# A decoder trunk in fp32: the down projection's pairs in seven products take one weight row per slot, and late loads go in pieces

## What is computed

```python
D_MODEL, SEQ, D_FF = 2048, 256, 8192

h = rms_norm(x, norm_mix_pre)
...
x = x + rms_norm(mixed @ w_out, norm_mix_post)
h = rms_norm(x, norm_mlp_pre)
u = jnp.square(jax.nn.relu(h @ w_up))
x = x + rms_norm(u @ w_down, norm_mlp_post)
```

## Time and profile before

| | |
|---|---|
| median of 3 runs | 1708.07 us (1706.89 to 1712.73) |
| profiled execution | 1709.83 us, span 1708.5 us |
| granted TensorE clock, mean | 0.998 |
| TensorE busy | 1686.1 us (99%), 8444 matmuls |
| weight loads of TensorE | 1397.4 us (82%) |
| VectorE busy | 1094.4 us (64%) |
| ScalarE busy | 879.3 us (51%) |
| GpSimd busy | 55.6 us (3%) |
| DMA | 341.12 MB, mean 200 GB/s; `w_down` loads: 128 of 512 KB, 4.6 us to landing |

### The profile page before, as it was taken

How to read it: one execution, slowest core, us unless ns; L and a number is a source line. 1 busy time by engine, 2 the same in 40 slices (tenths; PEclk the granted TensorE clock), 3 DMA queues, 4 the chain that set the end, 5 groups by cost and what they waited for, 6 DMA issues and landing times.

```text
span 1708.5 us, 23779 instructions
## 1 busy us (share of the span) xinstructions
PE 1686.1 (99%) x8444; PEld 1397.4 (82%) x8444; DVE 1094.4 (64%) x1508; ACT 879.3 (51%) x1318; POOL 55.6 (3%) x104
## 2 busy tenths in 40 slices
PE   9999999999999999999999999999999999999997
PEld 7888888888888888788888888887778888887886
DVE  6444456766655555565665667657878567568888
ACT  6444455766655655544344565445545444445553
POOL 1000011111100102000000000000000000000000
PEclk9999999999999999999999999999999999999999
DMA  8666665766666769668767656665556666666564
GB/s 267 197 188 185 193 189 146 197 174 169 173 176 186 207 207 299 189 184 291 272 202 237 216 184 185 189 183 184 194 187 210 198 186 186 187 231 199 187 204 146
DMA packets 169010, 341.12 MB, mean 200 GB/s; under 512 B 11488, under 2 KB 14512, under 8 KB 168144
## 3 DMA queue, kind: packets, MB, share of 16 engines
q1 hardware_dynamic: 163088, 319.27, 59.8%
q0 software_dynamic: 5696, 20.54, 5.1%
q10 hardware_dynamic: 128, 0.03, 0.0%
HBM read 329.21 MB, written 10.58 MB: 199 GB/s over the span
## 4 chain that ended last, share of the span: by engine, by line
PE 90%; DVE 5%; DMA 3%; issue 1%; ACT 0%; DVEq 0%; ACTq 0%
PE ps L1145 13%; PE ps L857 11%; PE ps L859 10%; PE ps L858 10%; PE ps L1147 6%; PE ps L672 6%; PE ps L674 6%; PE ps L673 6%; DMA raw<-in_w_down_dram 3%; PE ps L1181 3%; PE ps L1183 3%; PE ps L1182 3%; PE ps L1196 1%; PE ps L1197 1%; PE ps L1198 1%
## 5 line engine op out<-in xcount | busy, mean ns | idle before, releaser
L1758 DVE TENSOR_TENSOR w_lo<-raw,w_hi 128x1024 fp32r<-128x1024 f32 x524 | 635.8, 1224 | 476.6 <-ACT w_hi L1267 466.8
L1267 ACT ACTIVATE w_hi<-raw 128x1024 fp32r<-128x1024 f32 x547 | 575.7, 1057 | 574.7 <-PE ps L674 147.6
L1145 PE MATMUL ps<-h_all,w_hi 128*128 128x512 f32 x960 | 339.4, 399 | 0.0
L857 PE MATMUL ps<-w_hi,h_all 128*128 128x512 f32 (+1 forms) x800 | 314.6, 393 | 0.0
L859 PE MATMUL ps<-w_hi,h_all 128*128 128x512 f32 (+1 forms) x800 | 309.0, 386 | 0.0
L858 PE MATMUL ps<-w_lo,h_all 128*128 128x512 f32 (+1 forms) x800 | 308.7, 386 | 0.0
L1147 PE MATMUL ps<-h_all,w_lo 128*128 128x256 f32 x960 | 269.6, 281 | 0.0
L1145 PEld LDWEIGHTS ps<-h_all,w_hi 128*128 128x128 f32 x960 | 180.4, 188 | 45.0
L1147 PEld LDWEIGHTS ps<-h_all,w_lo 128*128 128x128 f32 x960 | 181.3, 189 | 0.1
L857 PEld LDWEIGHTS ps<-w_hi,h_all 128*128 128x128 f32 x800 | 150.2, 188 | 36.2 <-issue 7.5
L859 PEld LDWEIGHTS ps<-w_hi,h_all 128*128 128x128 f32 x800 | 150.1, 188 | 30.5
(11 more groups left out here) (357 smaller groups left out, 1941.4 us busy)
## 6 DMA issues: line engine op xcount, KB each, us to landing
raw<-in_w_in_dram SPq DMA_DIRECT2D x239, 512.0 KB, 3.9
raw<-in_w_down_dram SPq DMA_DIRECT2D x128, 512.0 KB, 4.6
raw<-in_w_up_dram SPq DMA_DIRECT2D x124, 512.0 KB, 4.2
raw<-in_w_out_dram SPq DMA_DIRECT2D x32, 512.0 KB, 4.1
bias<-bias_table POOLq DMA_DIRECT2D x72, 128.0 KB, 4.2
raw<-in_w_branch_b_dram SPq DMA_DIRECT2D x16, 512.0 KB, 5.7
raw<-in_w_branch_c_dram SPq DMA_DIRECT2D x16, 512.0 KB, 5.5
gate_dram<-stage SPq DMA_DIRECT2D x12, 512.0 KB, 6.3
```

The lines of the kernel that those rows point to most:

```text
L857: pe.matmul(acc, h_hi[:, kc, tok], w_hi[:, slot, k, 0:cols], start=kc == 0, stop=False)
L1145: pe.matmul(ps[:, bank + b, :], w_hi[:, j % RING, k, cols], h_all[:, kc, :, :].rearrange("p a n -> p (a n)"), start=kc == 0, stop=False)
L1267: act.activation(w_hi[:, slot, :, :], raw[:, slot, :, :], ACT.Copy).then_inc(sem("hi_ready"), 1)
L1758: dve.tensor_tensor(w_lo[:, slot, :, :], raw[:, slot, :, :], w_hi[:, slot, :, :].bitcast(F32), ALU.subtract).then_inc(sem("lo_ready"), 1)
```

## The change

The two units of a pair no longer hold a half of the columns each with both hidden rows, but one hidden row each with all 1024 columns (slot 2 the odd row, slot 3 the even one). The first sum needs slot 2 alone. Sums and plain rests are cut into smaller steps; the odd row's rest, in slot 2, counts `lo_ready` for the first unit of the pair, the rest of slot 3 for the second, and both `t_lo` count `t_lo_ready`. TensorE waits four times within a pair and does the three products with plain blocks first. For the first pair behind `up` both `t_lo` are made before `up_sum`. `mid_again` is loaded in eight pieces of 256 KB, one for each four units of `down(1, 0)`, and `gain_again` in four of 256 KB beside the first four. The first two gain products move from the slots of units 24 and 25 to those of 29 and 30. Blank lines are left out.

```diff
--- before.py
+++ after.py
@@ -563,10 +563,19 @@
             for c in range(2):
                 chunk(Pos(U0[f"up{h}"] + CH * c, 2 * CH, i), w_up_v, 0, CH, i * (2 * W) + (h * DFF // 2 + W * c))
+        def load_row(u, slot, view, kc, col):
+
+            sp.wait_ge(sem("lo_ready"), u.count(1 - RING))
+            sp.dma_start(raw[:, slot, :, :].rearrange("p k n -> p (k n)"), view[:, kc, col:col + 2 * W]).then_inc(
+                sem(f"raw_loaded{slot}"), 16)
+
         def down(h, part):
-            for j, (_, p, half) in enumerate(DOWN):
-                load(Pos(U0[f"down{h}"] + DOWN_UNITS * part + j), j % RING, w_down_v, 32 * h + 2 * p,
-                     2 * W * part + W * half)
+            for j, (seven_products, p, half) in enumerate(DOWN):
+                u = Pos(U0[f"down{h}"] + DOWN_UNITS * part + j)
+                if seven_products:
+                    load_row(u, j % RING, w_down_v, 32 * h + 2 * p + 1 - half, 2 * W * part)
+                else:
+                    load(u, j % RING, w_down_v, 32 * h + 2 * p, 2 * W * part + W * half)
         sp.wait_ge(sem("unit_used"), U0["out"])
         for j in range(RING):
@@ -650,9 +659,14 @@
             pool.dma_start(mid[:, t, :], x[0, t * P:(t + 1) * P, :]).then_inc(sem("x_again"), 16)
         pool.wait_ge(sem("mid_stored"), 16)
-        pool.wait_ge(sem("unit_used"), U0["down1"])
-        pool.dma_start(mid_again[:, :, :].rearrange("p t n -> p (t n)"), mid_dram).then_inc(sem("mid_back"), 16)
-        pool.dma_start(gain_again[:, :], bass.AP(norm_mlp_post.tensor, 0, [[0, P], [1, D]])).then_inc(sem("gain_loaded"), 16)
+        for t in range(2):
+            for b in range(4):
+                pool.wait_ge(sem("unit_used"), U0["down1"] + 4 * (4 * t + b))
+                cols = slice(W * b, W * b + W)
+                pool.dma_start(mid_again[:, t, cols], mid_dram[:, D * t + W * b:D * t + W * b + W]).then_inc(sem("mid_back"), 16)
+                if t == 0:
+                    gain = bass.AP(norm_mlp_post.tensor, W * b, [[0, P], [1, W]])
+                    pool.dma_start(gain_again[:, cols], gain).then_inc(sem("gain_loaded"), 16)
     @block.tensor
@@ -1201,18 +1215,21 @@
                 return product(seven_bank(h, number), a_hi, a_lo, b_hi, b_lo, n == 0, n == SEVEN - 1)
             low, high, odd = slice(0, P), slice(P, SEQ), 2 * p + 1
-            pe.wait_ge(sem("lo_ready"), U0[f"down{h}"] + DOWN_UNITS * part + 4 * n + 4)
-            own(1, u_hi[:, odd, low], u_lo[:, odd, low], w4_hi[:, 1, :], w4_lo[:, 1, :])
+            unit = U0[f"down{h}"] + DOWN_UNITS * part + 4 * n + 2
+            pe.wait_ge(sem("lo_ready"), unit + 1)
+            own(1, u_hi[:, odd, low], u_lo[:, odd, low], w4_hi[:, 0, :], w4_lo[:, 0, :]).then_inc(sem("unit_used"), 1)
+            pe.wait_ge(sem("lo_ready"), unit + 2)
+            product(sum_bank(h, 0, 0), u_hi[:, 2 * p, low], u_lo[:, 2 * p, low], w4_hi[:, 2, :], w4_lo[:, 2, :],
+                    False, False)
+            product(sum_bank(h, 1, 0), s_hi[:, n, 2, :], s_lo[:, n, 2, :], w4_hi[:, 3, :], w4_lo[:, 3, :],
+                    False, False).then_inc(sem("unit_used"), 1)
+            pe.wait_ge(sem("t_lo_ready"), 2 * number + 1)
             own(5, u_hi[:, odd, high], u_lo[:, odd, high], t_hi[:, 1, :], t_lo[:, 1, :])
             own(7, s_hi[:, n, 0, :], s_lo[:, n, 0, :], t_hi[:, 0, :], t_lo[:, 0, :]).then_inc(sem("t_used"), 1)
-            pe.wait_ge(sem("t_lo_ready"), number + 1)
+            pe.wait_ge(sem("t_lo_ready"), 2 * number + 2)
             own(6, s_hi[:, n, 1, :], s_lo[:, n, 1, :], t_hi[:, 2, :], t_lo[:, 2, :])
             product(sum_bank(h, 0, 1), u_hi[:, 2 * p, high], u_lo[:, 2 * p, high], t_hi[:, 3, :], t_lo[:, 3, :],
                     False, False).then_inc(sem("t_used"), 1)
-            product(sum_bank(h, 0, 0), u_hi[:, 2 * p, low], u_lo[:, 2 * p, low], w4_hi[:, 0, :], w4_lo[:, 0, :],
-                    False, False).then_inc(sem("unit_used"), 1)
-            product(sum_bank(h, 1, 0), s_hi[:, n, 2, :], s_lo[:, n, 2, :], w4_hi[:, 2, :], w4_lo[:, 2, :],
-                    False, False).then_inc(sem("unit_used"), 1)
         def down(h, part):
@@ -1656,16 +1673,16 @@
         def t_round(number, pair):
-            act.wait_ge(sem("t_sums"), 3 * number + 1 + 2 * pair)
+            act.wait_ge(sem("t_sums"), 4 * number + 2 + 2 * pair)
             act.activation(t_hi[:, 2 * pair:2 * pair + 2, :], t_sum[:, 2 * pair:2 * pair + 2, :], ACT.Copy).then_inc(
                 sem("t_hi_ready"), 1)
         def prepare(n):
-            if n - 1 in SEVEN_OF:
-                act.wait_ge(sem("raw_loaded3"), Pos(n).loads())
+            if n in SEVEN_OF:
+                act.wait_ge(sem("raw_loaded2"), Pos(n).loads())
                 act.wait_ge(sem("unit_used"), n + 1 - RING)
-                act.activation(w_hi[:, 3, 0, :], raw[:, 3, 0, :], ACT.Copy).then_inc(sem("hi_ready"), 1)
+                act.activation(w_hi[:, 2, 0, :], raw[:, 2, 0, :], ACT.Copy).then_inc(sem("hi_ready"), 1)
             else:
                 split(Pos(n), n % RING)
@@ -1693,7 +1710,7 @@
         def mix_first(h, part):
-            act.wait_ge(sem("unit_used"), U0[f"down{h}"] + DOWN_UNITS * part + SEVENS_END)
+            act.wait_ge(sem("t_used"), 2 * (12 * h + SEVEN * (part + 1)))
             act.wait_ge(sem("up_lo"), 8 * h + 8)
             act.wait_ge(sem("mix_v"), MIX_V[h][part])
             one = ps[:, seven_bank(h, 1), :]
@@ -2390,36 +2407,45 @@
                 dve.tensor_tensor(s_lo[:, part, :, :], s_sum[:, part, :, :], s_hi[:, part, :, :].bitcast(F32),
                                   ALU.subtract).then_inc(sem("s_lo_ready"), 1)
-        def weight_sums(n):
+        def first_sum(n):
             number = SEVEN_OF[n]
-            for b in range(2):
-                dve.wait_ge(sem(f"raw_loaded{2 + b}"), Pos(n + b).loads())
+            dve.wait_ge(sem("raw_loaded2"), Pos(n).loads())
             if number == 0:
                 dve.wait_ge(sem("mid_stored"), 16)
             wait(dve, sem("t_used"), 2 * number - 1)
             rows = plain_rows(raw)
-            dve.tensor_tensor(t_sum[:, 0:2, :], rows[:, 2:4, :], rows[:, 3:0:-2, :], ALU.subtract).then_inc(sem("t_sums"), 1)
-            dve.wait_ge(sem("t_sums"), 3 * number + 1)
+            dve.tensor_tensor(t_sum[:, 1, :], rows[:, 1, :], rows[:, 0, :], ALU.subtract).then_inc(sem("t_sums"), 1)
+
+        def second_sum(n):
+
+            dve.wait_ge(sem("raw_loaded3"), Pos(n + 1).loads())
+            rows = plain_rows(raw)
+            dve.tensor_tensor(t_sum[:, 0, :], rows[:, 3, :], rows[:, 1, :], ALU.subtract).then_inc(sem("t_sums"), 1)
+
+        def last_sums(n):
+
+            number = SEVEN_OF[n]
+            rows = plain_rows(raw)
+            dve.wait_ge(sem("t_sums"), 4 * number + 1)
             wait(dve, sem("t_used"), 2 * number)
-            dve.tensor_tensor(t_sum[:, 2, :], rows[:, 2, :], t_sum[:, 1, :], ALU.subtract).then_inc(sem("t_sums"), 1)
-            dve.wait_ge(sem("t_sums"), 3 * number + 2)
-            dve.tensor_tensor(t_sum[:, 3, :], rows[:, 0, :], t_sum[:, 2, :], ALU.subtract).then_inc(sem("t_sums"), 1)
-
-        def t_rest(number, pair, name):
+            dve.tensor_tensor(t_sum[:, 2, :], rows[:, 3, :], t_sum[:, 1, :], ALU.subtract).then_inc(sem("t_sums"), 1)
+            dve.wait_ge(sem("t_sums"), 4 * number + 3)
+            dve.tensor_tensor(t_sum[:, 3, :], rows[:, 2, :], t_sum[:, 2, :], ALU.subtract).then_inc(sem("t_sums"), 1)
+
+        def plain_rest(n, rows):
+
+            dve.wait_ge(sem("hi_ready"), n + 1)
+            wait(dve, sem("unit_used"), n + 1 - RING)
+            dve.tensor_tensor(plain_rows(w_lo)[:, rows, :], plain_rows(raw)[:, rows, :],
+                              plain_rows(w_hi)[:, rows, :].bitcast(F32), ALU.subtract).then_inc(sem("lo_ready"), 1)
+
+        def t_rest(number, pair):
             dve.wait_ge(sem("t_hi_ready"), 2 * number + pair + 1)
             part = slice(2 * pair, 2 * pair + 2)
             dve.tensor_tensor(t_lo[:, part, :], t_sum[:, part, :], t_hi[:, part, :].bitcast(F32), ALU.subtract).then_inc(
-                sem(name), 1)
-
-        def plain_rest(n):
-
-            dve.wait_ge(sem("hi_ready"), n + 2)
-            wait(dve, sem("unit_used"), n + 2 - RING)
-            rows = slice(0, 3)
-            dve.tensor_tensor(plain_rows(w_lo)[:, rows, :], plain_rows(raw)[:, rows, :],
-                              plain_rows(w_hi)[:, rows, :].bitcast(F32), ALU.subtract).then_inc(sem("lo_ready"), 1)
+                sem("t_lo_ready"), 1)
         def prepare(n, early=False):
@@ -2429,12 +2455,17 @@
                 split(Pos(n), n % RING)
                 return
             number = SEVEN_OF[n - 1]
-            if not early:
-                weight_sums(n - 1)
-            plain_rest(n - 1)
-            t_rest(number, 0, "lo_ready")
-            if not early:
-                t_rest(number, 1, "t_lo_ready")
+            if early:
+                plain_rest(n - 1, slice(0, 1))
```

(27 more changed lines are left out.)

## The result

The changed kernel takes 1690.82 us (median of 4 runs, 1690.44 to 1691.75) against 1707.48 us for the kernel before beside it (1705.21 to 1712.73). The ratio is 0.9899, 95% interval 0.9876 to 0.9922: 16.7 us less. A second comparison, made with the experiments, gave 1693.12 against 1708.08 us, a ratio of 0.9916 (0.9900 to 0.9931) and 15.0 us less. The forecast, 1692.4 us, lies between the two values of the changed kernel.

A forecast was written before the change was run, and what follows sets the result against it. TensorE, busy 99% of the span, was taken as the bound; 15.4 - 0.2 - 0.5 + 1.0 = 15.7 us off the profiled 1709.83 gives 1694.1, and from the median of 1708.07, 1692.4 us; range 1689.5 to 1701.5 with the rivals.

The forecast's parts named there:

- The waits as the place of the gain: Down projection: nine TensorE waits for `t_lo` cost 11.3 + 1.5 + 0.9 + 1.7 = 15.4 us, all to be won back.
- the half clock: Behind the longest wait, 3.1 us, TensorE runs 3.4 us at the lower clock, which costs 1.7 us.
- TensorE's two late starts: End of the program: TensorE waits for the last splits in VectorE's queue, about 2.0 us together.
- The ring as their cause: Slot 3's reload and the first `t_lo` need each other: 11.2 to 12.1 us against TensorE's 10.2; afterwards 8.5 to 10.4.
- The 8.8 us computed for VectorE: VectorE's work for a group of four units in the new order, as before, under TensorE's 10.2 us.
- First pairs: Behind `up`, 0.1 us of wait and 0.1 of restart charged once for both; in the second parts no wait left.
- The pieces: Late residual and gain loads, spread: critical load 1.2 us longer (0.4 to 1.7), leaving 0.4 us wait and 0.1 restart.
- The end: Gain products behind the last splits: VectorE becomes the bound, the end moves by 1.0 us (0 to 2.0).
- The slower rival: Loads of `w_down`: whole rows of 1024 columns land late, 8.4 us throughout, 30 us lost, 1722 us; chance 5%.
- an estimate from it: VectorE's fixed term per instruction: two more instructions would add 0.3 us a group, 9.2 instead of 8.8; forecast then 1693.6.
- Sum: Whole kernel: 15.4 - 0.2 - 0.5 + 1.0 = 15.7 us won.

The follow-up runs named there:

- experiment 4: Changed kernel, but TensorE begins a pair only when both plain rests and the first `t_lo` are there, as before; 1697.92 us, ratio 0.9940.
- experiment 5: Changed kernel with both slots of a pair reloaded one step of `lo_ready` later than they could be; 1717.45 us, ratio 1.0066.
- Experiment 2: Changed kernel with the two large loads of residual and gain of before in place of the pieces; 1695.15 us, ratio 0.9934.
- experiment 3: Changed kernel with the first two gain products back between the last splits; 1691.76 us, ratio 0.9914.
- experiment 9: The changed kernel again, nothing altered; 1693.12 us (1691.92 to 1693.64).
- experiment 10: Changed kernel with the first two gain products moved forward behind the splits of the last part's third and fourth group; 1692.47 us, ratio 0.9907.

## Why the prediction was right

**The waits as the place of the gain: right.** They cost 15.4 us by the sum and 15.3 us came back (4.9 + 1.8 + 6.7 in the first three parts; in the last, 1.9, while the other 2.0 of its 3.9 are TensorE's two late starts). The additions to the idle time, 0.16 and 0.1 us a wait and the half clock, were needed: idle time alone gives 11.3.

**The ring as their cause: right for five of the nine waits.** These five follow another pair and cost 9.4 us, the late loads' share of them included; experiments 4 and 5 separate the ring from the early start there. The 8.8 us computed for VectorE (8.9 measured), the handover of VectorE's idle to `t_used` and the period of 10.2 us stand in the rows. But the prediction took the ring for slower than it was. Its 11.2 to 12.1 us use the landings on the chain, which are among the slowest; the 24 loads of slot 3 landed in 4.5 us at the median before the change, which makes the old ring 10.0 us. Where it is above 10.2 us throughout, as in experiment 5, TensorE stops in 19 of the 20 pairs that follow another, and not in five.

**First pairs: right, cheaper.** The other four of the nine waits, at the first pair of each part, cost 5.9 us, and these are not the ring's. 0.07 us stayed of the 0.2 charged. With the early start taken away they cost 3.9 us (experiment 4), so the early start is worth 3.8 us of the 5.9; the other 2 us come with the rest of the change, at the two first pairs behind `up`, whose waits are 0.6 and 0.5 us in experiment 4 where they were 1.6 each.

**The pieces: the sum for that load was too high, and their worth went unsaid.** The load of slot 3 behind the first pieces took 6.0 us and not 6.9, and no wait stayed where 0.5 us were charged. What was mis-sized is the 5.7 us that the charge was added to: the load in the same place of the first half, with no pieces beside it, took 5.0 us in the changed kernel. The addition itself is 1.1 us, near the 1.2 taken. The Trainium skill ("DMA: Bandwidth & Descriptors", "Queues, rings and completion order") has an engine take turns between its queues by packets, which made the charge 1.7 us; the trace's 1.1 lies below that and above the 0.4 in proportion to the bytes. Loads beside the later pieces took up to 7.9 us, and TensorE did not wait for them, so the lead of the new ring bears the pieces. The prediction named the large loads as the maker of the longest wait but did not ask what would happen to them behind the new ring. Experiment 2 answers: they would still have cost 4.4 us.

**The end: right in kind, 1.3 us for 1.0.** The last part and the tail are 3.2 us shorter, less 1.9 of waits. VectorE did become the bound, and as the prediction had it, most of the gain is VectorE's earlier start: counted from the start of the last part and less the 1.9 us of waits, its step of the earlier trace rows at 1678.58 comes 1.1 us sooner (now at 1659.83). The rest is the place of the gain products, to which the prediction gave nothing: experiment 3 gives it 0.2 us. TensorE's two late starts, 2.0 us, are gone, but then VectorE holds the end by 0.8.

**The slower rival: refuted.** Whole rows of 1024 columns land in 4.6 us at the median, and all loads of `w_down` together in 4.5 (4.6 before). The Trainium skill ("VectorE: DVE Perf Modes", the TRN2 errata) has each VectorE instruction pay a fixed term; an estimate from it was 0.3 us more a group. The trace does not show it: ten steps took the 8.9 us that eight had taken.

**Sum.** 15.7 us forecast, 16.6 in the traces, 16.7 and 15.0 in the medians. The 0.9 us between the forecast and the traces are 0.5 + 0.1 of charges that did not fall due and 0.3 at the end. That the first medians agree with the traces to 0.1 us is luck: the medians carry the two forms of `up(0)` (last section) and the changing waits of the kernel before.

## What to carry to other kernels

When an engine that is busy for two thirds of the time still makes another wait, look for a ring: time from a buffer's landing to its next release, plus the landing, against the period of the bound engine, here 10.2 us. With 5.5 + 4.5 us some of the waits were there and their number changed; with 3.8 + 4.5 there was none; with 7.2 + 4.0 there was one in 19 of 20 pairs. Use the landings of all the loads for it, not those on the chain alone. Shortening the first term by the order of small steps cost nothing here, and the runs of the changed kernel spread over 3.2 us where those before spread over 10. A lead exists only where it has been built, so price each first round by itself, and large transfers that nobody is waiting for belong in pieces between the ones that somebody is.

## What the hardware showed besides

TensorE works through the looped part of `up(0)` in one of two ways, and the same kernel shows both. Busy times as in the earlier trace rows, counts of instructions in brackets; first the changed kernel, then the same kernel in experiment 9:

```profile
1060.00:1100.00 40.00, 40.00 (x233) 34.99 (x232) 28.13 (x31) 20.10 (x20) 0.00 (x0) 1.00 0.61 187
```

```profile
1060.00:1100.00 40.00, 40.00 (x228) 34.67 (x228) 28.75 (x31) 19.13 (x19) 0.00 (x0) 1.00 0.62 187
```

Both stretches have TensorE without a gap and at the full clock, yet 233 matmuls fit in one and 228 in the other: a pair of matmuls of 512 and 256 columns takes 0.347 or 0.353 us. It holds through all 768 matmuls, 133.1 or 135.7 us. Of the eleven traces besides that of before, six show the short form and five the long one, and the changed kernel and its copy one each; the kernel before has the long one. The same loop in `up(1)` showed 180.9 us, the long form, in every trace:

```profile
1400.00:1440.00 40.00, 40.00 (x228) 34.71 (x228) 28.76 (x31) 20.23 (x21) 0.00 (x0) 1.00 0.59 183
```

What sets it is open; it was not tried. The six runs of experiment 10, one kernel on one chip, fall into two groups, 1689.6 and 1690.0 us and 1692.4 to 1693.1, which speaks for the execution as what picks the form; no two traces of one kernel on one chip show it. It would explain such steps of about 2.6 us between runs of one kernel, and it is most of why the two profiled spans differ by 19.0 us where the medians differ by 16.7. Between two traces of the long form, that of before and that of experiment 9, the spans differ by 16.2 us.

The lower clock of TensorE followed a single stop of 3.1 us, and in experiment 2 two stops of 2.2 us in all within 3.6 us, the longer one 1.5 us. In experiment 5 stops of up to 1.5 us that stood alone had no lower clock behind them, and the two pairs that held two stops each (1.4 and 1.5 us, 0.4 and 1.5 us) had.
